# The down products of the first expert, cut into two of 64 rows each

## What is computed

```python
def expert_block(args):
    tok, e = args
    xb = h_pad[tok]
    return (jax.nn.silu(xb @ w_gate[e]) * (xb @ w_up[e])) @ w_down[e]
```

## Time and profile before

| | before |
|---|---|
| median of 2 runs | 1472.91 us |
| the profiled execution | 1473.06 us |
| its span, first to last instruction | 1471.1 us |
| TensorE matmuls (PE) busy | 1455.7 us, 99% |
| TensorE weight loads (PEld) busy | 1263.1 us, 86% |
| VectorE (DVE) busy | 1227.7 us, 83% |
| ScalarE (ACT) busy | 969.5 us, 66% |
| mean granted TensorE clock | 0.999 of full speed |

### The profile page before, as it was taken

How to read it: one execution, slowest core, us unless ns; L and a number is a source line. 1 busy time by engine, 2 the same in 40 slices (tenths; PEclk the granted TensorE clock), 3 DMA queues, 4 the chain that set the end, 5 groups by cost and what they waited for, 6 DMA issues and landing times.

```text
span 1471.1 us, 20293 instructions
## 1 busy us (share of the span) xinstructions
PE 1455.7 (99%) x7821; PEld 1263.1 (86%) x7821; DVE 1227.7 (83%) x1211; ACT 969.5 (66%) x921; POOL 126.1 (9%) x139
## 2 busy tenths in 40 slices
PE   8999999999999999999999999999999999999998
PEld 8979999999997888888888888888888888788887
DVE  7988555554698799999999888888889889999886
ACT  5745333344476777777777777777777777777774
POOL 3522000000024200001000000000000102200000
PEclk9999999999999999999999999999999999999999
DMA  9726544455253599999999999999999999999991
GB/s 350 165 91 211 172 166 151 168 172 172 93 134 114 226 375 398 362 396 382 391 376 381 378 386 371 401 364 373 383 363 388 395 388 385 405 373 360 374 378 65
DMA packets 68601, 440.48 MB, mean 299 GB/s; under 512 B 9568, under 2 KB 13600, under 8 KB 17184
## 3 DMA queue, kind: packets, MB, share of 16 engines
q1 hardware_dynamic: 60464, 424.69, 76.2%
q0 software_dynamic: 5120, 13.37, 3.0%
q10 hardware_dynamic: 2928, 1.18, 0.4%
HBM read 432.12 MB, written 7.09 MB: 299 GB/s over the span
## 4 chain that ended last, share of the span: by engine, by line
PE 65%; DVE 2%; ACT 1%; issue 1%; POOL 0%; DVEq 0%; ACTq 0%; POOLq 0%
PE bank L962 60%; PE bank L998 2%; PE bank L757 1%; DVE w_lo L2083 1%; PE bank L952 0%; PE bank L943 0%; ACT h_tok_hi L1293 0%; DVE r_tok L2047 0%; PE bank L1060 0%; PE bank L1061 0%; DVE w_lo L2099 0%; ACT x_rows L1293 0%; PE bank L1080 0%; ACT w_hi L1350 0%; ACT w_hi L1361 0%
## 5 line engine op out<-in xcount | busy, mean ns | idle before, releaser
L2083 DVE TENSOR_TENSOR w_lo<-ring,w_hi 128x2048 fp32r<-128x2048 f32 x320 | 731.0, 2289 | 79.8 <-ACT w_hi L1350 77.0
L1350 ACT ACTIVATE w_hi<-ring 128x2048 fp32r<-128x2048 f32 x320 | 613.3, 1918 | 162.5 <-PE bank L962 162.3
L962 PE MATMUL bank<-w_hi,x_hi 128*128 128x512 f32 x896 | 354.2, 395 | 1.2 <-DVE w_lo L2083 0.8
L962 PE MATMUL bank<-w_hi,x_lo 128*128 128x512 f32 x896 | 349.4, 390 | 0.0
L962 PE MATMUL bank<-w_lo,x_hi 128*128 128x512 f32 x896 | 348.5, 389 | 0.0
L962 PEld LDWEIGHTS bank<-w_hi,x_hi 128*128 128x128 f32 x896 | 168.3, 188 | 36.8 <-issue 1.6
L962 PEld LDWEIGHTS bank<-w_hi,x_lo 128*128 128x128 f32 x896 | 168.2, 188 | 35.8
L609 PE MATMUL bank<-x_hi,w_hi 128*128 128x290 f32 x656 | 196.4, 299 | 1.3 <-DVE w_lo L1425 1.2
L962 PEld LDWEIGHTS bank<-w_lo,x_hi 128*128 128x128 f32 x896 | 168.4, 188 | 33.1
L609 PE MATMUL bank<-x_lo,w_hi 128*128 128x290 f32 x656 | 195.1, 297 | 0.0
L609 PE MATMUL bank<-x_hi,w_lo 128*128 128x290 f32 x656 | 194.6, 297 | 0.0
(11 more groups left out here) (332 smaller groups left out, 1756.1 us busy)
## 6 DMA issues: line engine op xcount, KB each, us to landing
ring<-in_w_e_gate SPq DMA_DIRECT2D x112, 1024.0 KB, 7.2
ring<-in_w_e_up SPq DMA_DIRECT2D x112, 1024.0 KB, 7.1
ring<-in_w_e_down SPq DMA_DIRECT2D x112, 1024.0 KB, 7.3
ring<-in_w_in SPq DMA_DIRECT2D x15, 1024.0 KB, 5.0
ring<-in_w_ff_gate SPq DMA_DIRECT2D x14, 1024.0 KB, 4.9
ring<-in_w_ff_up SPq DMA_DIRECT2D x14, 1024.0 KB, 4.9
ring<-in_w_ff_down SPq DMA_DIRECT2D x14, 1024.0 KB, 4.8
ring<-in_w_out SPq DMA_DIRECT2D x8, 1024.0 KB, 9.1
```

Of the source, the lines that this page charges most:

```text
L962: ins = mm(out, x, w[slot][:, columns], start=(first and n == 0), stop=(last and n == 2), skip_group_check=True)
L1350: A(w_hi[(CUT0 + p) % SPLIT][:, :], ring[(START + p) % SLOTS][:, :], ACT.Copy).then_inc(hi_done, 1)
L2083: V.tensor_tensor(w_lo[(CUT0 + p) % SPLIT][:, :], ring[(START + p) % SLOTS][:, :], w_hi[(CUT0 + p) % SPLIT][:, :].bitcast(F32), ALU.subtra ...
```

## The change

The item function of TensorE gets a flag, `half_rows`, which is set for item 0 alone. With it, `down` calls a new function, `down_by_rows`. It cuts each product of 128 rows into two of 64 rows: one over partitions 0 to 63, one over partitions 64 to 127. Each of them still has 512 columns. A call is made of two turns of 12 such half products. In a turn, neighbours in the queue alternate between bank 4 and bank 5 and between the row halves: in turn 0 the lower half goes with bank 4 and the upper half with bank 5, and in turn 1 the other way round. After each turn TensorE waits for its own last product (`rows_added`), so that no two row halves write one bank at the same time. The only turn without such a wait is the last one of the item. `chunk_done`, which the last product of a call raised before, is now raised by an instruction of its own after the second wait (in the last call by the last product, as before). Nothing changes on the other engines, nor in the items behind.

```diff
+            def down_by_rows(g, half, p, first, last):
+
+                slot = (CUT0 + p) % SPLIT
+                for turn in range(2):
+                    for f in range(GB // 2):
+                        ff = half * (GB // 2) + f
+                        for n, (x, w) in enumerate(((a_hi, w_hi), (a_hi, w_lo), (a_lo, w_hi))):
+                            for d in range(2):
+                                rows, at = slice(64 * (d ^ turn), 64 * (d ^ turn) + 64), f * D_MODEL + d * 512
+                                ins = mm(bank[4 + d][:, :], x[g % 2][rows, ff, :], w[slot][rows, at:at + 512],
+                                         start=(first and turn == f == n == 0),
+                                         stop=(last and turn == f == 1 and n == 2), skip_group_check=True)
+                    if turn == 0 or not last:
+                        half_sums[0] += 1
+                        ins.then_inc(rows_added, 1)
+                        pe.wait_ge(rows_added, half_sums[0])
+                if not last:
+                    pe.sem_inc(chunk_done, 1)
+                return ins
...
+                    if half_rows:
+                        stop = g == E_GROUPS - 1 and half == 1
+                        last = down_by_rows(g, half, p, g == 0 and half == 0, stop)
+                        if stop:
+                            last.then_inc(chunk_done, 1)
+                        return
...
-                item(2 * j, 0, 4 * j, "hold", tabled=True)
+                item(2 * j, 0, 4 * j, "hold", tabled=True, half_rows=j == 0)
```

More of the change, by code:

```diff
@@ L327, in build @@
         ones_ready, setup = sem("ones_ready"), sem("setup")
+        rows_added = sem("rows_added")
         half_in, half_hi = sem("half_in"), sem("half_hi")
@@ L964, in parts @@
                 return ins
+            half_sums = [0]
+            def down_by_rows(g, half, p, first, last):
[16 more added lines that the diff above has]
+                return ins
             gather_first()
@@ L974, in _, with item @@
                 pe.sem_inc(s, 2 * TABLED)
-            def item(i, e, x_from, after, x_next=None, tabled=False):
+            def item(i, e, x_from, after, x_next=None, tabled=False, half_rows=False):
                 n_scat = i if after == "one" else N_EXPERTS - 1
@@ L1006, in down @@
                     pe.wait_ge(lo_done, i * CPI + CUT0 + p + 1)
+                    if half_rows:
[4 more added lines that the diff above has]
+                        return
                     for f in range(GB // 2):
                         ff = half * (GB // 2) + f
+                        first, stop = g == 0 and ff == 0, g == E_GROUPS - 1 and ff == GB - 1
                         for d in range(2):
@@ L1011, in down @@
                             last = parts(bank[4 + d][:, :], a_hi[g % 2][:, ff, :], a_lo[g % 2][:, ff, :], p,
-                                         slice(at, at + 512), g == 0 and ff == 0,
-                                         g == E_GROUPS - 1 and ff == GB - 1)
+                                         slice(at, at + 512), first, stop)
                     last.then_inc(chunk_done, 1)
```

## The result

The changed kernel takes 1487.38 us (median of 2 runs, 1487.22 to 1487.53) against 1472.91 before. That is 14.5 us more, 1.0%. The ratio on record is 1.0095, with a 95% interval of 1.0079 to 1.0111, so the change is slower, clear of the noise, and by less than 2%. The profiled execution took 1487.53 us.

The account below looks back on a forecast made before the run. TensorE's queue was taken as the bound, busy 114.08 of 114.10 us in item 0. Turns +12.3, row changes +0.7, last turn -0.1 made +12.9 on 1473.06: 1486 us, own range 1482 to 1492, stated 1481 to 1524.

Parts of the forecast that it names:

- the rival: Item 0's half products run one after the other, not together: +48.0 us, 1521 us; chance 0.25.
- Half products share the array's time: Item 0's `down`: two halves run at once, 0.227 us for a pair, as for one full product.
- open loads: Rival: halves share, but a half's next load starts only after its product has streamed; +28.3 us, 1501 us; chance 0.10.
- The partner's load: At each turn's start the second half's load follows the first, so the partner starts 0.11 us later.
- A wait: At each turn's restart: first load 0.11 us in the open, last record 0.39 to its end, signal 0.06.
- The increments: 13 added instructions that raise `chunk_done` in item 0; listed among the additions, with no time of their own in the sum.
- The changes of rows: From 128-row to 64-row products, seven times in item 0, about 0.1 us lost each: +0.7 us.
- The way back to 128 rows: From 64 to 128 rows after `down`: six are behind a wait and free; the last turn, without wait, saves about 0.1 us.
- Cover: VectorE and ScalarE get more time in item 0, but that gives nothing back; nothing later shifts relative to TensorE.
- signs to look for: In the changed trace, the new line's product starts should alternate at about 0.11 us, six pairs in 1.36 us.
- one reading of the earlier trace: Whole kernel before the change: the longest single wait shown for TensorE was read as 1.2 us in total.
- its doubled loads: Argument against the change: two loads per pair, 0.22 us, just under the pair's 0.227; halving rows makes no load cheaper.

Follow-up runs that it names:

- the run with full products: The change with six full 128-row products in a turn instead of half products, same 27 waits and 13 increments: 1485.11 us, +11.75 us on the kernel before.
- the run without own increments: The change with a call's last product raising chunk_done and TensorE waiting for that, the 13 own instructions gone, 27 waits kept: 1484.28 us.
- all five runs: Orders of half products: six and six 1503.16, by twos 1487.46, six and six without waits 1480.62, by threes 1487.19, twelve and twelve without waits 1498.56 us.

## Why the prediction was right

The forecast was 1486 us, its own range 1482 to 1492 and the stated one, widened for the rival, 1481 to 1524; 1487.4 was measured, by the mechanism that was named. Point by point:

- **Half products share the array's time.** Right: pairs follow at 0.23 us, about 0.003 more than full products, and half products without waits cost 2.7 us. That the halves might come one by one (1521 us) or with open loads (1501 us) is excluded by the same rows.
- **The partner's load** was put into the sum with 0.11 us in each turn, 3.1 us. This step failed: two loads of different halves last 0.19 us together, so the partner does not start later. It was only the edge of the range that had this case.
- **A wait** was put at 0.11 + 0.39 + 0.06, less 0.227. The row at 525.66 has its start 0.46 us after the last one, where 0.45 was said, and then the load. In the run with full products, 11.75 us less the increments' 3.1 to 3.6 leaves 8.2 to 8.7 us for 27 waits, 0.30 to 0.32 each against 0.33. By the lengths of item 0, 11.96 - 2.74 = 9.22 us, it is 0.34.
- **The increments** were named (13 instructions) and then had no term in the sum. That was the second error: 2.7 us by the length of item 0 and 3.1 to 3.6 by the medians, 0.21 to 0.27 each. An instruction of its own behind a wait is not free on an engine that is the bound, since the next product is behind it.
- **The changes of rows** were taken at about 0.1 us beyond the turn's load; the rows have 0.32 - 0.227 = 0.09. The way back to 128 rows behind a wait was called free. It is not quite: the first load lies in the open there, too. At the start of the piece at 531.31 the trace has two product starts 0.31 us apart, 0.08 more than normal, and 0.11 more behind the short holds of the run without own increments; that is 0.4 to 0.6 us for the six.
- **Cover.** Right: items 1 to 7 with the tail take 852.09 instead of 851.92 us, and nothing gave the delay back. The 0.17 us are mostly the open load after the last change of rows.

The two errors are of one size and opposite sign, and so the sum held: 12.9 - 3.1 + 2.7 = 12.5 us against 13.67 in item 0. The 0.003 us more for each pair (28 turns x 5 x 0.003 = 0.4) and the six open loads (about 0.5) make up most of what remains. That the forecast came so close owes something to that luck.

One of the signs to look for was wrong, too: starts were to alternate at 0.11 us, and they are together. And one reading of the earlier trace rows was: the largest sum shown there is 1.6 us, not 1.2, and the longest single wait 0.9. Both are small beside the span, and nothing in the argument hung on them.

## What to carry to other kernels

Cutting a product whose rows already fill the array into two row halves gains nothing, since a pair takes as long as the full product. It costs what is needed to keep the halves out of each other's banks: here 0.3 us for each wait of TensorE for itself, 0.2 to 0.25 for each increment of its own behind such a wait, and 0.2 for each open change of rows. Where products are short in rows to begin with, the sharing is real, loads included, and two or three neighbours of one half in a row do no harm. Let the last product raise the semaphore, and give each half a bank of its own. Here that would take two more banks and an addition of the halves' sums; the run with fixed banks left that out and mixed the sums, so no run has the price of it.

## What the runs showed of the hardware that was not expected

Products of different row halves leave the order of the queue. An upper product started beside the third lower one with three more lower ones before it in the queue, and beside the ninth of twelve, again with three before it; blocks of two and of three cost nothing (1487.46 and 1487.19 us against 1487.38), blocks of six 16 us. A reach of three waiting products fits all five runs. What holds them was not seen. Whether the reach counts products or also their loads, and whether it depends on the products' size or type, was not tried. The Trainium skill has it otherwise (TensorE: Matmul & The Clock Gate, "The mechanism"): there, matmuls start and end strictly in program order. Here that is not so across row halves. Its few nanoseconds between the starts of neighbours in different halves agree with the rows of this case, whose pairs start within 0.01 us (up to 0.04 in a turn behind an increment of its own).

Two loads for different halves take the time of one, 0.19 us for both. So the reason that the prediction gave against the change, its doubled loads, carries no weight at this size of product.
